# Two modulation pieces of the second block's layer 1, moved from an output projection to the feed-forward behind it

## The chip, the cores and the metric

The kernel runs on one core of one Trainium2 chip. The time of a run is the device time of one execution in microseconds, from start to end. The kernel before was timed three times: 1384.77, 1386.67 and 1389.09 us, median 1386.67 us.

## The reference, cut to what matters

Two transformer blocks in float32, batch 1, 256 tokens, width 1024. The first has causal attention and a recurrent branch, then a feed-forward. The second has two layers: layer 0 with a neighbourhood attention and a gated feed-forward, layer 1 with a latent attention and a mixture of experts. Both layers of the second block are modulated by vectors computed from a conditioning vector c:

```python
c_act = jax.nn.silu(c)
for i in range(DEPTH_2):
    mod = c_act @ w_ada[i] + b_ada[i]            # 1024 -> 6 * 1024
    sh_a, sc_a, g_a, sh_f, sc_f, g_f = jnp.split(mod, 6, axis=-1)
    h = _modulate(x, sh_a, sc_a)                 # rmsnorm(x) * (1 + sc_a) + sh_a
    m = attention of this layer (h)
    x = x + g_a * m
    h = _modulate(x, sh_f, sc_f)
    x = x + g_f * (_swiglu(h) if i == 0 else _moe(h))
```

The product `c_act @ w_ada[i]` doesn't depend on x. Its weights are 24 MB for each layer, so it may be computed at any time before the layer that uses it, as long as someone reads the weights and multiplies them.

## The kernel before, in words

**Splitting in two.** Every weight matrix comes in as float32 chunks of 1 MB (`raw`, 4 slots, loaded by SP's queue). ScalarE rounds a chunk to a high part (`whi`, line 1178) and VectorE takes the difference as a low part (`wlo`, line 1672), each in two halves. TensorE multiplies high by high, low by high and high by low (lines 681 to 683 where the weights are stationary or 694 to 698 where the activations run past them). Of `whi` and `wlo` there are two slots, so a chunk can be split only once TensorE is done with the chunk two before it.

**The modulation.** `mod` of a layer is made of 24 pieces (`ADA_CHUNKS`). Piece j is 128 rows of `w_ada` by 2048 columns (1 MB, 128 partitions by 2048), loaded by SP into one of two slots of `ada` (line 546, `load_ada`). VectorE multiplies it by a column of c and adds it to an accumulator of 128 x 2048 (`modulate_part`): the first of each eight pieces by a tensor_scalar (line 1760), the other seven by a scalar_tensor_tensor (line 1763). Pieces 0 to 7 go to `acc_first`, 8 to 15 to `acc_mid`, 16 to 23 to `acc_ends`. TensorE later sums an accumulator over partitions with one-column matmuls (line 789), and VectorE adds the bias (line 1812, `shifts`).

**What sets the order.** Nothing is planned at run time. Three tables say after which weight chunk a piece is loaded by SP and accumulated by VectorE, each entry for layer 0 and layer 1 of the second block: `ADA_MIX` for the output projection ahead of a feed-forward, `ADA_UP` for the 11 steps of the feed-forward's first product (`GU_STEPS`), and `ADA_DOWN`, the first piece that goes with the 11 chunks of its second product (`DN_CHUNKS`); all pieces from there to 23 go with one chunk each. Entry 1 is worked beside the second block's layer 0: the output projection `W_NAO` of the neighbourhood attention (4 chunks), the first product of its feed-forward `W_GU`, and the second product `W_DN2`. The result is wanted at the norm ahead of the latent attention (`norm(4, ...)`).

**SP at this place.** `load_ffn` waits for `ada_free1`, because the `ada` slots have held attention biases until the neighbourhood attention's last head is done. Then it issues the first four chunks of `W_GU` in turn, with the pieces of `ADA_MIX` among them, and goes on:

```python
if layer:
    sp.wait_ge(sem("ada_free1"), 1)
for c in range(NRAW):
    if c < len(ADA_MIX[layer]):
        load_ada(layer, ADA_MIX[layer][c])
    load(gu + c)
```

**VectorE at this place.** `down` splits a chunk and then accumulates a piece, and everything stands in one instruction stream ahead of the norm:

```python
ve.sem_inc(sem("ada_free1"), 1)
down(W_NAO, 4, 1, ADA_MIX[1], begun=1)
norm(3, halves(W_GU), halves(W_GU + 1), sc_f, sh_f, residual_gate(2, W_GU))
gate_up_silu(W_GU)
down(W_DN2, DN_CHUNKS, 1, range(ADA_DOWN[1], ADA_CHUNKS))
shifts(1, (0, 1, 3), 0, 2)
```

**The norm.** Tokens are in two tiles of 128, t = 0 and t = 1. TensorE ends an output projection with its last two chunks for t = 0 (then `tile_done`) and for t = 1. In `norm`, VectorE runs for t = 0 the gated residual (lines 1957 and 1958), splits the first half of the next stage's first chunk, waits for ScalarE's sum of squares (line 1195), and scales the rows (line 1690); ScalarE, in its own stream, splits both halves of that chunk (line 1178) ahead of the squares. TensorE turns the scaled rows by transposes (line 726). Ahead of and between the transposes of `norm(3)` and `norm(4)` stand matmuls without use (line 717, `fill`): in `norm(3)` two of them before t = 0, five between t = 0 and t = 1 and one behind; a float32 matmul shows as two rows. VectorE and ScalarE modulate the turned tiles (lines 1695 and 1207) and split them (1705 and 1213), and the first product starts.

Of the kernel before, what the change touches and what calls it, by code (L numbers as in the profile page):

```python
# [94 lines left out]
ADA_COLS = 2 * D  # L95
ADA_FIRST = KT
ADA_IN = 6
ADA_MIX = [[6, 7], [0, 1]]
ADA_UP = [{j: [7 + j] for j in range(1, 10)}, {}]
for _j in range(GU_STEPS):  # L100
    _n = 2 + _j + _j // 3
    ADA_UP[1][_j] = [_n, _n + 1] if _j % 3 == 2 else [_n]
ADA_DOWN = [ADA_UP[0][9][-1] + 1, ADA_UP[1][GU_STEPS - 1][-1] + 1]

# [147 lines left out]
def blocks(nc, a, out):  # L252

    ctx = ExitStack()
    with ctx:
# [19 lines left out]
        def sem(name):  # L275
            if name not in sems:
                sems[name] = ctx.enter_context(nc.semaphore(name))
            return sems[name]
# [240 lines left out]
        def _(sp):  # L519
            def load(c):  # L520
                ck = Chunk(c)
                if c >= NRAW:
                    sp.wait_ge(lo_done, 2 * (c - NRAW + 1))
                k, n = chunk_shape(c)
                sp.dma_start(view(raws[ck.slot], k, n), dram_chunk(c)).then_inc(raw_in[ck.slot], 16)
# [14 lines left out]
            def load_ada(layer, j):  # L540

                g = layer * ADA_CHUNKS + j
                sp.wait_ge(ada_used, g + 1)
                part, k = j // KT, j % KT
                src = a["w_ada_2"][layer][k * P:(k + 1) * P, part * ADA_COLS:(part + 1) * ADA_COLS]
                sp.dma_start(ada[:, g % NADA], src).then_inc(ada_in[g % NADA], 16)

            def load_ffn(gu, layer):
# [3 lines left out]
# [4 lines that stand above are left out]
# [1109 lines left out]
        def _(ve):  # L1665
# [47 lines left out]
            def norm(s, first, second, scale, shift=None, residual=None, between=None):  # L1713

                if s:
                    residual(0)
                    first(0)
                    normed(s, 0)
                    if s < 3:
                        first(1)  # L1720
                    residual(1)
                else:
                    normed(0, 0)
                    normed(0, 1)
                ve.wait_ge(sem("turned"), TURNED0[s] + 1)
                modulate(s, 0, 0, 4, scale, shift)
                if s:
                    normed(s, 1)
                else:
                    first(0)  # L1730
                ve.wait_ge(sem("aT_hi"), HI0[s] + 1)
                own.mark(low(0, 4, slice(0, P)))
                if between:
                    between()
                ve.wait_ge(sem("turned"), TURNED0[s] + 3)
                modulate(s, 1, 0, 2, scale, shift)
                modulate(s, 1, 2, 4, scale, shift)
                for n in range(2):
                    ve.wait_ge(sem("aT_hi"), HI0[s] + 2 + n)
                    low(2 * n, 2 * n + 2, slice(P, S)).then_inc(sem("aT_ready"), 1)  # L1740
                for n in range(2, 4):
                    ve.wait_ge(sem("aT_hi"), HI0[s] + 2 + n)
                    low(2 * n, 2 * n + 2).then_inc(sem("aT_ready"), 1)
                if not 0 < s < 3:
                    first(1)
                second(0)
                second(1)

            def halves(c):
                return lambda q: split(c, (q,))  # L1750
# [195 lines left out]
            def residual_gate(s, first):  # L1946

                gate = gate_row[(s - 2) // 2][(s - 2) % 2]

                def residual(t):  # L1950
                    if t == 0:
                        ve.wait_ge(sem("tile_done"), s + 1)
                    else:
                        ve.wait_ge(mm_done, 2 * first)
                    b = OUT_BANKS[s][t]
                    o = ps[:, b:b + 2, :].rearrange("p b n -> p (b n)")
                    own.link(ve.tensor_tensor(xn[:, t], o, gate, ALU.mult))
                    ve.tensor_tensor(x[:, t], x[:, t], xn[:, t], ALU.add).then_inc(sem("x_ready"), 1)
                return residual

            def down(first, chunks, layer=None, pieces=(), also=None, begun=0):

                for c in range(begun, chunks):
                    if also:
                        also(c)
                    if c < chunks - 2:
                        split(first + c + 2)
                    if c - begun < len(pieces):
                        modulate_part(layer, pieces[c - begun])
# [8 lines left out]

            down(W_OUT, 4, 0, ADA_MIX[0], begun=1)
            sh_a, sc_a, sh_f, sc_f = (mod[:, n * KT:(n + 1) * KT] for n in range(4))  # L1980
# [86 lines left out]
# [3 lines that stand above are left out]
# [344 lines left out]
```

## Time and profile before

| | before |
|---|---|
| median of three runs | 1386.67 us (1384.77 to 1389.09) |
| the profiled execution | 1393.49 us, of which the span is 1391.7 us |
| TensorE, matmuls | 1307.6 us busy, 94% of the span |
| VectorE | 1078.3 us busy, 77% |
| ScalarE | 834.5 us busy, 60% |
| DMA | 349.13 MB, mean 251 GB/s |
| mean granted TensorE clock | 0.967 of full speed |

The span runs from the first to the last instruction; the rest of the execution's time lies around it. Times in the rows are microseconds from the start of the span. A busy TensorE isn't TensorE at its peak, since matmuls are pipelined and overlap in the rows. The bracket behind a row tells how long the engine had been idle before it and what ended the wait.

### The profile page before, as it was taken

The numbers are of one execution on the slowest core, as the hardware profiler recorded it, in microseconds if no ns is written. First come the engines' busy times: TensorE is split into PE (matmuls) and PEld (weight loads), VectorE is DVE, ScalarE is ACT, GpSimd is POOL, SyncE is SP. The second block draws the span as 40 slices with busy tenths as digits, with TensorE's granted clock in tenths as the row PEclk, the third lists the DMA queues.
The fourth block names the chain that finished last, engine by engine and source line by source line (L and its number), as shares of the span: only waits on it lengthen the run. The fifth ranks groups of instructions, "written<-read, shape, count | busy, mean of one in ns | idle before, by whom it ended". The sixth has DMA issues, their size and how long they took to land.

```text
span 1391.7 us, 20370 instructions
## 1 busy us (share of the span) xinstructions
PE 1307.6 (94%) x7608; PEld 1141.8 (82%) x7608; DVE 1078.3 (77%) x1199; ACT 834.5 (60%) x1104; POOL 72.3 (5%) x102
## 2 busy tenths in 40 slices
PE   6989999998999799999777988999999999999996
PEld 5977999886988599998665567888888888889894
DVE  6888899878655677776635457889888888989888
ACT  5766666535655444433425655777777777777764
POOL 0010000003512000000001300000000000000000
PEclk9999999999999899999988997999999999999999
DMA  9945776699730689898232034999989998999992
GB/s 321 340 183 192 277 272 242 239 309 205 184 122 31 242 278 312 298 352 295 81 117 79 10 113 155 340 327 341 339 320 350 314 353 321 355 315 362 317 348 82
DMA packets 192890, 349.13 MB, mean 251 GB/s; under 512 B 23892, under 2 KB 161439, under 8 KB 186551
## 3 DMA queue, kind: packets, MB, share of 16 engines
q1 hardware_dynamic: 189713, 343.41, 71.9%
q10 hardware_dynamic: 2934, 4.24, 0.9%
q8 instruction: 45, 0.74, 0.2%
q0 software_dynamic: 176, 0.56, 0.1%
q14 instruction: 22, 0.18, 0.0%
HBM read 347.12 MB, written 1.06 MB: 250 GB/s over the span
## 4 chain that ended last, share of the span: by engine, by line
PE 84%; DVE 7%; ACT 5%; issue 1%; DMA 1%; POOL 0%; ACTq 0%; SPq 0%; DVEq 0%
PE ps L1143 11%; PE ps L681 8%; PE ps L682 8%; PE ps L683 8%; PE ps L1113 8%; PE ps L1115 7%; PE ps L1114 7%; PE ps L694 5%; PE ps L696 5%; PE ps L698 5%; DVE wlo L1672 1%; PE ps L1084 1%; PE ps L812 1%; PE ps L1055 1%; DVE alo L1705 1%
## 5 line engine op out<-in xcount | busy, mean ns | idle before, releaser
L1178 ACT ACTIVATE whi<-raw 128x1024 fp32r<-128x1024 f32 (+2 forms) x210 | 217.5, 1052 | 245.4 <-PE ps L683 136.3
L1672 DVE TENSOR_TENSOR wlo<-raw,whi 128x1024 fp32r<-128x1024 f32 (+2 forms) x210 | 253.0, 1229 | 117.5 <-ACT whi L1178 114.1
L681 PE MATMUL ps<-ahi,whi 128*128 128x256 f32 x960 | 276.6, 288 | 8.8 <-DVE alo L1705 8.2
L682 PE MATMUL ps<-alo,whi 128*128 128x256 f32 x960 | 273.4, 285 | 0.0
L683 PE MATMUL ps<-ahi,wlo 128*128 128x256 f32 x960 | 273.3, 285 | 0.0
L1680 DVE TENSOR_TENSOR wlo<-raw,whi 128x1792 fp32r<-128x1792 f32 (+1 forms) x96 | 199.9, 2090 | 24.6 <-ACT whi L1191 22.9
L1191 ACT ACTIVATE whi<-raw 128x1792 fp32r<-128x1792 f32 (+1 forms) x96 | 168.6, 1757 | 63.5 <-PE ps L1115 34.6
L681 PEld LDWEIGHTS ps<-ahi,whi 128*128 128x128 f32 x960 | 186.0, 194 | 14.2 <-issue 9.4
L682 PEld LDWEIGHTS ps<-alo,whi 128*128 128x128 f32 x960 | 186.0, 194 | 0.7 <-issue 0.7
L683 PEld LDWEIGHTS ps<-ahi,wlo 128*128 128x128 f32 x960 | 186.1, 194 | 0.0
L1113 PE MATMUL ps<-whi,hchi 128*128 128x448 f32 x352 | 131.4, 373 | 3.4 <-DVE hclo L2244 2.8
L1115 PE MATMUL ps<-whi,hclo 128*128 128x448 f32 x352 | 129.9, 369 | 0.0
L1114 PE MATMUL ps<-wlo,hchi 128*128 128x448 f32 x352 | 129.8, 369 | 0.0
L694 PE MATMUL ps<-whi,ahi 128*128 128x256 f32 (+3 forms) x216 | 66.2, 342 | 15.2 <-DVE wlo L1672 6.2
L1113 PEld LDWEIGHTS ps<-whi,hchi 128*128 128x128 f32 x352 | 66.7, 189 | 13.1 <-issue 4.3
L1680 DVE TENSOR_TENSOR alo<-raw,ahi 128x1792 fp32r<-128x1792 f32 (+1 forms) x32 | 66.9, 2090 | 8.3 <-ACT ahi L1191 8.3
L1115 PEld LDWEIGHTS ps<-whi,hclo 128*128 128x128 f32 x352 | 66.6, 189 | 6.0
L1680 DVE TENSOR_TENSOR wlo<-ada,whi 128x1792 fp32r<-128x1792 f32 (+2 forms) x32 | 60.5, 1891 | 14.0 <-ACT whi L1191 14.0
L1114 PEld LDWEIGHTS ps<-wlo,hchi 128*128 128x128 f32 x352 | 66.7, 189 | 5.7
L1680 DVE TENSOR_TENSOR alo<-ada,ahi 128x1792 fp32r<-128x1792 f32 (+2 forms) x32 | 60.3, 1886 | 8.6 <-ACT ahi L1191 8.6
L1191 ACT ACTIVATE ahi<-ada 128x1792 fp32r<-128x1792 f32 (+2 forms) x32 | 51.0, 1594 | 25.8 <-PE ps L1115 19.6
L696 PE MATMUL ps<-wlo,ahi 128*128 128x256 f32 (+3 forms) x216 | 64.4, 333 | 0.0
(321 smaller groups left out, 2536.7 us busy)
## 6 DMA issues: line engine op xcount, KB each, us to landing
raw<-in_moe_w_gu SPq DMA_DIRECT2D x96, 896.0 KB, 6.0
ada<-in_w_ada SPq DMA_DIRECT2D x48, 1024.0 KB, 6.9
raw<-in_moe_w_down SPq DMA_DIRECT2D x32, 1024.0 KB, 6.9
ada<-in_moe_w_gu SPq DMA_DIRECT2D x32, 896.0 KB, 6.5
raw<-in_w_up SPq DMA_DIRECT2D x22, 1024.0 KB, 5.2
raw<-in_ffn_w_gu SPq DMA_DIRECT2D x22, 1024.0 KB, 9.9
ada<-in_moe_w_down SPq DMA_DIRECT2D x16, 1024.0 KB, 7.3
raw<-in_na_w_qkv SPq DMA_DIRECT2D x12, 1024.0 KB, 7.8
```

The source lines that it names most:

```text
L681: pe.matmul(o, h[:, k, cols], bhi[:, k], start=(k == 0), stop=False)
L682: pe.matmul(o, h[:, k, cols], blo[:, k], start=False, stop=False)
L683: m = pe.matmul(o, l[:, k, cols], bhi[:, k], start=False, stop=(k == KT - 1))
L694: pe.matmul(o, bhi[at_k][:, tok], h[:, k, n0:n0 + n], start=first, stop=False)
L1113: pe.matmul(o, hchi[:, kk], h[:, k], start=(kk == 0), stop=False)
L1114: pe.matmul(o, hchi[:, kk], l[:, k], start=False, stop=False)
L1115: m = pe.matmul(o, hclo[:, kk], h[:, k], start=False, stop=(kk == KT - 1))
L1143: m = pe.matmul(ps[:, 4 + n, :], lhs[:, k0 + k], rhs[:, k, n * 512:(n + 1) * 512], start=(k0 + k == 0 and rhs is h and lhs is gchi), stop= ...
L1178: act.activation(part_of(whi[ck.half], c, q), part_of(raws[ck.slot], c, q), ACT.Copy).then_inc(hi_done, 1)
L1191: act.activation(whi[ck.half][:, 0:k * n], raws[ck.slot][:, 0:k * n], ACT.Copy).then_inc(moe_hi, 1)
L1672: ve.tensor_tensor(part_of(wlo[ck.half], c, q), part_of(raws[ck.slot], c, q), part_of(whi[ck.half], c, q).bitcast(F32), ALU.subtract).then ...
L1680: ve.tensor_tensor(wlo[ck.half][:, 0:k * n], raws[ck.slot][:, 0:k * n], whi[ck.half][:, 0:k * n].bitcast(F32), ALU.subtract).then_inc(moe_ ...
```

## The change

Pieces 0 and 1 of entry 1 leave the output projection `W_NAO`; the first product's step j now has the pieces numbered two lower, and the second product begins with piece 14 in place of 16, so it has ten pieces with its eleven chunks in place of eight.

```diff
-ADA_MIX = [[6, 7], [0, 1]]
+ADA_MIX = [[6, 7], []]
 ADA_UP = [{j: [7 + j] for j in range(1, 10)}, {}]
 for _j in range(GU_STEPS):
-    _n = 2 + _j + _j // 3
+    _n = _j + _j // 3
     ADA_UP[1][_j] = [_n, _n + 1] if _j % 3 == 2 else [_n]
 ADA_DOWN = [ADA_UP[0][9][-1] + 1, ADA_UP[1][GU_STEPS - 1][-1] + 1]
```

The instructions of TensorE, ScalarE and GpSimd stay the same and in the same order; VectorE and SP change at these places.

VectorE, between the last split of `W_NAO` and the first tile of `norm(3)` (a piece of the difference; `acc_first_66` is the accumulator of pieces 0 to 7):

```order
 L1825 TENSOR_TENSOR alo<-ps,ahi 128x256
 L1672 TENSOR_TENSOR wlo<-raw,whi 128x1024 x2
-L1760 TENSOR_SCALAR acc_first_66<-ada,vecs 128x2048
-L1763 SCALAR_TENSOR_TENSOR acc_first_66<-ada,vecs,acc_first_66 128x2048
 L1957 TENSOR_TENSOR xn<-ps,gates 128x1024
 L1958 TENSOR_TENSOR x<-x,xn 128x1024
```

The two accumulations that stood between the split and the gated residual are gone from there.

SP, from the loads of the attention's output weights on. Before:

```order
L525 DMA raw<-in_na_w_o 128x2x1024 x4
L546 DMA ada<-in_w_ada 128x2048
L525 DMA raw<-in_ffn_w_gu 128x8x256
L546 DMA ada<-in_w_ada 128x2048
L525 DMA raw<-in_ffn_w_gu 128x8x256 x3
L546 DMA ada<-in_w_ada 128x2048
```

And now:

```order
L525 DMA raw<-in_na_w_o 128x2x1024 x4
L525 DMA raw<-in_ffn_w_gu 128x8x256 x4
L546 DMA ada<-in_w_ada 128x2048
L525 DMA raw<-in_ffn_w_gu 128x8x256
L546 DMA ada<-in_w_ada 128x2048
```

The first four chunks of the feed-forward are issued one behind the other, ahead of any piece.

VectorE, the end of the second product and the start of `norm(4)`. Before:

```order
L1763 SCALAR_TENSOR_TENSOR acc_ends<-ada,vecs,acc_ends 128x2048
L1672 TENSOR_TENSOR wlo<-raw,whi 128x1024 x2
L1763 SCALAR_TENSOR_TENSOR acc_ends<-ada,vecs,acc_ends 128x2048
L1672 TENSOR_TENSOR wlo<-raw,whi 128x1024 x2
L1812 SCALAR_TENSOR_TENSOR mod<-ps,vecs 128x8 x3
L1957 TENSOR_TENSOR xn<-ps,gates 128x1024
L1958 TENSOR_TENSOR x<-x,xn 128x1024
```

And now:

```order
L1763 SCALAR_TENSOR_TENSOR acc_ends<-ada,vecs,acc_ends 128x2048
L1672 TENSOR_TENSOR wlo<-raw,whi 128x1024 x2
L1763 SCALAR_TENSOR_TENSOR acc_ends<-ada,vecs,acc_ends 128x2048 x2
L1812 SCALAR_TENSOR_TENSOR mod<-ps,vecs 128x8 x3
L1957 TENSOR_TENSOR xn<-ps,gates 128x1024
L1958 TENSOR_TENSOR x<-x,xn 128x1024
```

Two more accumulations, of pieces 22 and 23, now stand directly between the last split of the second product and the start of the next norm.

## Rows read from the trace of the kernel before

**Rows 1.** The page, part 4: the chain that ended last, by engine.
```profile
PE 84%; DVE 7%; ACT 5%; issue 1%; DMA 1%; POOL 0%; ACTq 0%; SPq 0%; DVEq 0%
```

**Rows 2.** Windows: from:to, length, busy PE, PEld, DVE, ACT, POOL, granted clock, DMA.
```profile
465.00:470.00 5.00, 0.00 (x0) 0.00 (x0) 4.56 (x5) 1.44 (x3) 0.00 (x0) 0.67 1.10 348
470.00:475.00 5.00, 4.11 (x11) 2.77 (x12) 4.43 (x8) 2.11 (x5) 0.00 (x0) 0.50 0.66 255
```

**Rows 3.** Timeline of VectorE at norm(3): start, length, instruction, idle before and releaser.
```profile
457.03 1.29 DVE L1760 TENSOR_SCALAR acc_first<-ada,vecs 128x2048 f32<-128x2048 f32 x1 [2.22 <-DMA ada<-in_w_ada]
463.59 2.35 DVE L1763 SCALAR_TENSOR_TENSOR acc_first<-ada,vecs,acc_first 128x2048 f32<-128x2048 f32 x1 [5.28 <-DMA ada<-in_w_ada]
465.86 1.22 DVE L1957 TENSOR_TENSOR xn<-ps,gates 128x1024 f32<-128x1024 f32 x1
467.11 1.22 DVE L1958 TENSOR_TENSOR x<-x,xn 128x1024 f32<-128x1024 f32 x1
```

**Rows 4.** Timeline of TensorE, end of the projection to the first product.
```profile
456.18 0.62 PE L698 MATMUL ps<-whi,alo 128*128 128x512 f32 x2
...
462.15 1.88 PE L717 MATMUL ps<-cst 128*128 128x512 f32 x4
470.89 1.97 PE L726 MATMUL ps<-cst,xn 128*128 128x128 f32 x8 [6.86 <-DVE xn L1690]
472.65 6.62 PE L717 MATMUL ps<-cst 128*128 128x512 f32 x10
479.10 1.04 PE L726 MATMUL ps<-cst,xn 128*128 128x128 f32 x8
...
481.58 0.36 PE L681 MATMUL ps<-ahi,whi 128*128 128x256 f32 x1 [0.59 <-DVE alo L1705]
```

**Rows 5.** Timeline, SP's loads at norm(3) and ScalarE, who waits for them.
```profile
452.02 0.34 SPq L546 DMA_DIRECT2D ada<-in_w_ada  x1
452.40 0.43 SPq L525 DMA_DIRECT2D raw<-in_ffn_w_gu  x1
...
461.01 2.00 ACT L1178 ACTIVATE whi<-raw 128x1024 fp32r<-128x1024 f32 x2 [6.13 <-DMA raw<-in_ffn_w_gu]
468.37 1.06 ACT L1195 ACTIVATE xn<-x 128x1024 f32<-128x1024 f32 x1 [5.36 <-DVE x L1958]
```

**Rows 6.** The page, part 6: issues, KB each, median us from issue to landing.
```profile
raw<-in_w_up SPq DMA_DIRECT2D x22, 1024.0 KB, 5.2
```

**Rows 7.** Timeline of TensorE in norm(4), and a window of the same place.
```profile
681.21 1.09 PE L726 MATMUL ps<-cst,xn 128*128 128x128 f32 x8 [0.53 <-DVE xn L1690]
687.04 1.09 PE L726 MATMUL ps<-cst,xn 128*128 128x128 f32 x8 [1.23 <-DVE xn L1690]
...
684.00:688.00 4.00, 2.77 (x12) 1.36 (x12) 2.61 (x8) 2.48 (x5) 0.00 (x0) 1.00 0.00 0
```

**Rows 8.** Windows in the first and in the second product of the feed-forward.
```profile
520.00:540.00 20.00, 20.00 (x169) 20.00 (x169) 15.88 (x15) 9.44 (x11) 0.00 (x0) 1.00 0.97 341
...
640.00:660.00 20.00, 20.00 (x88) 16.05 (x87) 17.07 (x11) 7.44 (x7) 0.00 (x0) 1.00 0.99 376
```

**Rows 9.** Timeline of VectorE at the end of the second product.
```profile
663.51 2.35 DVE L1763 SCALAR_TENSOR_TENSOR acc_ends<-ada,vecs,acc_ends 128x2048 f32<-128x2048 f32 x1
...
667.96 1.23 DVE L1672 TENSOR_TENSOR wlo<-raw,whi 128x1024 fp32r<-128x1024 f32 x1 [0.97 <-ACT whi L1178]
...
674.26 1.22 DVE L1957 TENSOR_TENSOR xn<-ps,gates 128x1024 f32<-128x1024 f32 x1 [4.85 <-PE ps L698]
675.52 1.23 DVE L1958 TENSOR_TENSOR x<-x,xn 128x1024 f32<-128x1024 f32 x1
```

**Rows 10.** Timeline of ScalarE in norm(4): the squares of tile 0.
```profile
678.71 1.04 ACT L1195 ACTIVATE xn<-x 128x1024 f32<-128x1024 f32 x1
```

**Rows 11.** Issue to landing of all pieces (first row) and of all raw chunks.
```profile
DMA to landing us min/median/max: 4.8/6.9/12.5
...
DMA to landing us min/median/max: 4.3/7.0/15.4
```

## The prediction

> **What bounds the kernel now.** I read the chain that ended last first: 84% of it is TensorE, 7% VectorE and 5% ScalarE [rows 1]. So work taken off VectorE is worth something only in the few stretches where TensorE stands still for it, and next I looked for the stretch that the change touches. The windows show it: between 465 and 470 us TensorE did nothing, and in the next window it ran at a granted clock of 0.50 [rows 2], which is 1.2 GHz, the lower of its two levels.
>
> The timelines tell who it waited for. VectorE sat idle until the first piece had landed (457.03), accumulated it, sat idle for another 5.28 us until the second had landed (463.59), and only then took up the gated residual at 465.86 [rows 3]. That residual needed nothing but TensorE's t = 0 part of the projection, whose last matmuls end at 456.18 + 0.62 = 456.8 [rows 4]. So both pieces, 3.6 us of work with the waits around them, stand on the path for about 9 us: the transposes of tile 0 begin at 470.89, and TensorE had been idle for 6.86 us [rows 4]. Then TensorE pays again: at the low clock its transposes and the five matmuls without use took until 479.10.
>
> **Part 1: the pieces leave the projection.** VectorE can begin the residual at about 456.85. The same step in norm(4) begins right behind TensorE's t = 0 part, with no piece in between [rows 9]. It ends two instructions later, 467.11 + 1.22 - 465.86 = 2.5 us [rows 3], at 459.3.
>
> Next is ScalarE, which must split both halves of the first feed-forward chunk (2.00 us) before it squares [rows 5]. That chunk landed at 461.01, 8.6 us after its issue, with one piece issued ahead of it and one behind it. Now it is issued first, at 452.02 where the piece was issued; SP's wait for the attention still stands ahead of it. When does it land? The nearest rows give: a piece at the head of the same burst, 457.03 - 452.02 = 5.0 us [rows 3, 5]; chunks of the same shape in the first feed-forward, 5.2 us median [rows 6]; and the old landing less the distance between the two old landings, 8.6 - 4.0 = 4.6 us. At the other end stands the full 8.6 to 9.0 us, if the place in the queue were worth nothing. I take 5.5 us, near the 5.2 but with some allowance for the three chunks right behind it: 457.5.
>
> Then ScalarE splits until 459.5 and squares; from its squares to the transposes took 470.89 - 468.37 = 2.5 us [rows 4, 5]. So tile 0 could be turned at 462.0. But TensorE itself is busy with t = 1 and the two fills until 462.15 + 1.88 = 464.0 [rows 4], and the next group of instructions begins 0.2 us before the last one's modelled end, as between fills and transposes at 479.10. So the transposes begin at 463.9 instead of 470.9: **7.0 us**. The cover is good for a landing until 463.9 - 2.5 - 2.0 = 459.4, 7.4 us after issue.
>
> **Part 2: the clock.** From the transposes of tile 0 to those of tile 1 it took 479.10 - 470.89 = 8.2 us, and the fills at the low clock ended that time (6.6 us for ten rows, where four rows took 1.88 at full clock, so 4.7 for ten) [rows 4]. With a TensorE that doesn't stand still for 7 us ahead of it, I take the same stretch of norm(4) as the model: 687.04 - 681.21 = 5.8 us, at clock 1.00 with gaps of 0.53 and 1.23 us [rows 7]. Its weight chunk is narrower, by about 0.2 us of ScalarE. So 6.0 us: **2.2 us** more. The bounds are 0, if the clock falls all the same, and 2.4. From tile 1 on, to the first product at 481.58, I expect the same spacing as before.
>
> A rule speaks against this part. The Trainium skill, TensorE: Matmul & The Clock Gate, section on psum-queue depth-cycling, says that short idle times between groups of matmuls can make the clock swing between its levels. By it the 2.2 us would not come and the sum would be 7.0. The row of norm(4) speaks against the rule here, so it is a rival and no more.
>
> **Part 3: the feed-forward's first product.** It has the same number of pieces in each step, numbered two lower. Step 0 gets a first piece of eight (1.29 us) where it had a 2.35 us one. TensorE is busy 20.00 of 20.00 us in this stage and VectorE 15.9 [rows 8], so this is worth 0. The loads keep their places in SP's queue, except that chunks 0 to 3 come one or two transfers earlier and the first piece lands behind them; it is wanted only some 9 us after the first product has begun. If this cover were gone, the price would be the 2.35 us of one piece.
>
> **Part 4: the second product.** Ten chunks carry a piece instead of eight. Per chunk TensorE needs 5.6 us and VectorE 2.4 + 2.35 = 4.8, so VectorE keeps up; in the window with a piece for every chunk TensorE is busy all the time, at 376 GB/s [rows 8]. Two chunks more at that rate cost 0. The first chunk carries a 2.35 us piece instead of a 1.28 us one, with two chunks of lead: 0.
>
> The end is the delicate place. Piece 22 follows the last split at 667.96 + 1.23 = 669.2 and ends at 671.5. Piece 23 is loaded when piece 21 has freed its slot, which is at 663.51 + 2.35 = 665.9 [rows 9]. With the fastest landing of a piece, 4.8 us, it is there at 670.7, ahead of its turn; with the median of 6.9 us at 672.8 [rows 11]. So it is accumulated by 673.8 or by 675.1. Behind it stand the small shift sums, some 0.5 us, and the residual, which began at 674.26 [rows 9]. That residual has room: ScalarE takes up the squares only at 678.71, when it has split the next chunk [rows 10], and the residual ended at 675.52 + 1.23 = 676.75, so there are 2.0 us of slack. The cost is 0 for both landings. At the longest landing, 12.5 us [rows 11], it is 678.4 + 2.35 + 0.5 = 681.2 against the 676.2 allowed: 5.0 us. I take 0: only one chunk stands ahead of this piece in the queue, issued when the chunk two before it was split, one 5.6 us step earlier.
>
> **The sum.** 7.0 + 2.2 + 0 + 0 = 9.2 us. No other stage starts by the clock on the wall, so what is won is carried to the end. The profiled execution took 1393.49 us around a span of 1391.7; I expect 1384.3 of it. The three timed runs have their median at 1386.67, 6.8 us below the profiled one, and reach over 4.3 us. I take the same 9.2 us off that median: **1377.5 us**. A measurement can tell about 0.3%, 4.2 us, from no change.
>
> **The rivals.**
>
> A. **The chunk is what keeps the norm, not the piece.** If the order in the queue is worth nothing, it still lands at 461.0, and the transposes begin at 461.0 + 2.0 + 2.5 = 465.5: 5.4 us, with the clock 7.6 us. For it: ScalarE did wait 6.13 us for it, and three 1 MB chunks follow it at once. Against it: 4.0 us lay between the landings of the piece and of the chunk, so the queue does work mostly in order. Result 1379 to 1381 us. One page bears on the size: the Trainium skill, DMA: Bandwidth & Descriptors, table of specifications, gives line rate from 512 bytes on, so by it the chunk with its 1 KB rows should land as fast as the piece, at 457.0; the 4.0 us between the two landings are rather more than one megabyte at the measured 348 GB/s (3.0 us).
>
> B. **The clock doesn't stay up.** The transposes begin at 463.9 but tile 1 follows 8.2 us later: 7.0 us, 1379.7 us. For it: the norm remains a place with short gaps, and the rule above. Against it: norm(4).
>
> C. **The time is won at norm(3) and mostly given back in front of norm(4)**, by a late piece 23 of 5.0 us as worked out above: net 4.2 us or less, 1382.5 us or more. For it: in the second product the DMA share is 0.99 [rows 8], and pieces have taken up to 12.5 us. Against it: those long landings came in bursts like the one at 452.
>
> D. **Slower.** The same mechanism with a heavier price: VectorE runs in order, so the shift sums, both residuals and the splits for the latent attention are queued behind its wait for piece 23, and TensorE waits for them. With a landing of 15.4 us, the longest of any weight chunk [rows 11], the residual begins at 684.1, 7.9 us late. TensorE then stands still long enough to fall to the low clock as it did at 465, which cost 0.9 us on the transposes and 1.9 on the fills: 10.7 us against 9.2, so 1388 us. It decides from a landing of about 14 us on. Nothing in rows of this stage is near that.
>
> **How the numbers follow.** The forecast (8 to 10.5 us won) has a chance of 0.62. A has 0.12 and B 0.12; both are still faster by more than 0.3%. C and the case that no gain shows at the end at all have 0.10, D has 0.04. So: faster 0.86, within 0.3% 0.10, slower 0.04. The range goes from 1374.0, which is a gain of 10.5 us and the 2 us by which the lowest timed run lies under the median, to 1382.5, where C begins; it takes in A and B.
>
> **What would show it.** In the changed profile the residual at line 1957 begins near 456.9 and line 1763 no longer stands ahead of it; ScalarE's wait for the chunk ends near 457.5; the transposes (726) follow at 463.9 and 469.9 with a clock of 1.00 between them; the first product begins at 472.3. At the end of the second product two accumulations follow the last split, and the squares of norm(4) begin as far behind TensorE's t = 1 part as before. I am wrong if ScalarE's wait ends past 459.4 (A), if tile 1 follows tile 0 by 8 us (B), or if the residual of norm(4) begins more than 2 us behind tile_done (C, D).

## The result, and the profile after

The changed kernel takes 1380.94 us (median), the kernel before 1388.17 us in the same series: a ratio of 0.9939, 95% interval 0.9923 to 0.9955. The ratio leaves out one slow run of the changed kernel (1622.28 us at a granted clock of 0.741). By the ratio that is 8.5 us less, by the two medians 7.2; forecast were 9.2 us and a time of 1377.5. A second series gave 0.9938 (0.9915 to 0.9961). The profiled execution of the changed kernel took 1380.68 us around a span of 1378.9.

Two profiled executions also differ where nothing was changed: in this one the projection ahead of norm(3) ends 2.8 us sooner than in the one shown before (the first fill at 459.37 instead of 462.15), since the clock was a little higher between 300 and 400 us. The two spans lie 12.8 us apart, which is more than the times show: 2.8 us of it lie ahead of norm(3), 8.9 between its first fill and tile 1 of norm(4), and 1.1 behind that. So I read everything from the first fill of norm(3) on, the first row of line 717. The timeline of TensorE in the changed kernel (start, length, instruction, idle before and releaser) answers to [rows 4]:

```profile
459.37 1.88 PE L717 MATMUL ps<-cst 128*128 128x512 f32 x4
461.32 1.09 PE L726 MATMUL ps<-cst,xn 128*128 128x128 f32 x8
462.25 4.46 PE L717 MATMUL ps<-cst 128*128 128x512 f32 x10
467.31 1.09 PE L726 MATMUL ps<-cst,xn 128*128 128x128 f32 x8 [0.60 <-DVE xn L1690]
...
469.85 0.36 PE L681 MATMUL ps<-ahi,whi 128*128 128x256 f32 x1 [0.59 <-DVE alo L1705]
```

From the first fill to the transposes of tile 0 it is now 1.95 us, where it was 8.74; from those to the transposes of tile 1 it is 5.99 us, where it was 8.21; and on to the first product 2.54, where it was 2.48. Together 10.48 us instead of 19.43, so 8.95 us less. The ten rows of five fills take 4.46 us instead of 6.62: the clock.

What VectorE, ScalarE and SP do there, three timelines of the changed kernel and the landing of the first chunk (last row: KB, us from issue to landing), answers to [rows 3, 5]:

```profile
454.06 1.23 DVE L1957 TENSOR_TENSOR xn<-ps,gates 128x1024 f32<-128x1024 f32 x1 [1.99 <-PE ps L698]
455.32 1.23 DVE L1958 TENSOR_TENSOR x<-x,xn 128x1024 f32<-128x1024 f32 x1
...
456.91 2.01 ACT L1178 ACTIVATE whi<-raw 128x1024 fp32r<-128x1024 f32 x2 [4.78 <-PE ps L698]
458.82 1.04 ACT L1195 ACTIVATE xn<-x 128x1024 f32<-128x1024 f32 x1
...
449.27 5.22 SPq L525 DMA_DIRECT2D raw<-in_ffn_w_gu  x4
...
raw<-in_ffn_w_gu SPq DMA_DIRECT2D x1, 1024.0 KB, 5.2
```

The residual no longer waits for a landing but for TensorE's t = 0 part. The thing to see is the second bracket: ScalarE's split, which used to wait 6.13 us for the chunk's landing, now waits for TensorE (4.78 <-PE). The chunk has landed at 449.27 + 5.2 = 454.5, 2.4 us before the split, but the slot of `whi` that ScalarE writes is still being read. And the residual is over at 456.55, 2.3 us before ScalarE takes its squares at 458.82.

The window from 465 to 470 us, in which TensorE had done nothing before, answers to [rows 2]; its columns are the same (the clock is the third number from the end):

```profile
465.00:470.00 5.00, 3.81 (x15) 1.71 (x15) 3.21 (x8) 2.99 (x8) 0.00 (x0) 1.00 0.02 10
```

The end of the second product, timelines of VectorE, ScalarE and TensorE, answers to [rows 7, 9, 10]:

```profile
656.25 1.23 DVE L1672 TENSOR_TENSOR wlo<-raw,whi 128x1024 fp32r<-128x1024 f32 x1 [0.97 <-ACT whi L1178]
657.40 4.80 DVE L1763 SCALAR_TENSOR_TENSOR acc_ends<-ada,vecs,acc_ends 128x2048 f32<-128x2048 f32 x2
662.12 0.30 DVE L1812 SCALAR_TENSOR_TENSOR mod<-ps,vecs 128x8 f32<-128x8 f32 x3
662.57 1.23 DVE L1957 TENSOR_TENSOR xn<-ps,gates 128x1024 f32<-128x1024 f32 x1
...
667.00 1.04 ACT L1195 ACTIVATE xn<-x 128x1024 f32<-128x1024 f32 x1
...
669.50 1.09 PE L726 MATMUL ps<-cst,xn 128*128 128x128 f32 x8 [0.53 <-DVE xn L1690]
675.33 1.09 PE L726 MATMUL ps<-cst,xn 128*128 128x128 f32 x8 [1.23 <-DVE xn L1690]
```

Pieces 22 and 23 run back to back in 4.80 us, so piece 23 had landed: it was issued at 654.17 and took 4.9 us, so it was there at 659.1, some 0.7 us before its turn. The residual has lost its wait for TensorE (4.85 us before), but begins as far ahead of the first fill of norm(4) as before, 5.38 us against 5.40. The transposes of tile 1 follow those of tile 0 after 5.83 us, as before. From the first product of the feed-forward to the transposes of norm(4) it is 199.65 us (469.85 to 669.50), before it was 199.63. From the first fill in norm(3) to tile 1 in norm(4) the kernel has gained 8.9 us (215.96 instead of 224.89). The second pair of traces has 10.65 us there (214.38 instead of 225.03); the 1.7 us more are scatter of the clock in the second product, of which the last section tells.

### The profile page after: what moved, and what is told of

It reads as the page before. It is cut to its first block, busy times and chain, and to the rows that moved or that the text cites. A ratio compares the mean times of both kernels' runs of the same rounds, so it can differ in the third digit from the quotient of the medians.

```text
span 1378.9 us, 20370 instructions
## 1 busy us (share of the span) xinstructions
PE 1301.3 (94%) x7608; PEld 1138.0 (83%) x7608; DVE 1078.2 (78%) x1199; ACT 834.8 (61%) x1104; POOL 73.7 (5%) x102
## 4 chain that ended last, share of the span: by engine, by line
PE 86%; DVE 6%; ACT 5%; issue 1%; POOL 0%; DMA 0%; ACTq 0%; DVEq 0%
PE ps L1143 11%; PE ps L681 8%; PE ps L682 8%; PE ps L683 8%; PE ps L1113 8%; PE ps L1115 8%; PE ps L1114 8%; PE ps L694 6%; PE ps L696 5%; PE ps L698 5%; PE ps L1084 1%; DVE wlo L1672 1%; PE ps L812 1%; PE ps L1055 1%; PE ps L1091 1%
## 5 line engine op out<-in xcount | busy, mean ns | idle before, releaser
L1191 ACT ACTIVATE ahi<-raw 128x1792 fp32r<-128x1792 f32 (+1 forms) x32 | 56.1, 1752 | 12.8 <-PE ps L1143 6.7
```

What stands on the lines that cost most here:

```text
L1191: act.activation(whi[ck.half][:, 0:k * n], raws[ck.slot][:, 0:k * n], ACT.Copy).then_inc(moe_hi, 1)
```

## The experiments

**One piece at a time, and loads apart from work.** The first four kernels change one thing each. Pieces 0 and 1 loaded as before, but accumulated in the feed-forward (changed kernel, SP's part of the code):

```diff
                 for c in range(NRAW):
-                    if c < len(ADA_MIX[layer]):
+                    if layer and c < 2:
+                        load_ada(layer, c)
+                    elif c < len(ADA_MIX[layer]):
                         load_ada(layer, ADA_MIX[layer][c])
                     load(gu + c)
...
+                        if layer == 0 or n > 1:
                             load_ada(layer, n)
```

> Changed kernel, but pieces 0 and 1 are still LOADED among the first four chunks, as before; VectorE accumulates them in the feed-forward. I read the distance from the first use-less matmul (line 717) of norm(3) to the first product (line 681): 19.4 us before, 10.5 us in the changed kernel. Theory 1, the gain came from VectorE's order, and the place in the queue costs only what the chunk lands later: ScalarE gets its first chunk about 1.3 us later than TensorE's slot allows (1.1 us ahead of the first fill instead of 2.5), so 11.8 us, total gain against before 7.6 us. Rival, the queue place was what mattered: the loads are as before, so the distance stays above 16 us and the gain under 4 us.

Measured: ratio 0.9957 (0.9939 to 0.9975). In its trace (lines are numbered 3 higher) ScalarE and TensorE show:

```profile
459.53 2.00 ACT L1181 ACTIVATE whi<-raw 128x1024 fp32r<-128x1024 f32 x2 [6.38 <-DMA raw<-in_ffn_w_gu]
...
460.39 1.88 PE L720 MATMUL ps<-cst 128*128 128x512 f32 x4
463.94 1.09 PE L729 MATMUL ps<-cst,xn 128*128 128x128 f32 x8 [1.67 <-DVE xn L1693]
```

The first product follows the first fill after 12.08 us (472.47), near the 11.8 of theory 1. So in the changed kernel the old place of the loads costs 1.6 us of the 8.95, through the chunk that then lands 8.8 us after its issue; the order on VectorE is the other 7.3. The clock stays up behind an idle time of 1.67 us. All this is read from the trace: the interval of the time overlaps that of the changed kernel, here and in the next two experiments.

The work without the loads (changed kernel, VectorE):

```diff
             down(W_NAO, 4, 1, ADA_MIX[1], begun=1)
+            xf, c0 = x.rearrange("p t n -> p (t n)"), vec("c")[:, 0:1]
+            own.link(ve.tensor_scalar(acc_first1, xf, c0, None, ALU.mult))
+            own.link(ve.scalar_tensor_tensor(acc_first1, xf, c0, acc_first1, ALU.mult, ALU.add))
```

> Changed kernel plus two operations on VectorE at the old place of the pieces, of the same size and kind (tensor_scalar and scalar_tensor_tensor, 128 x 2048, 3.6 us together), which read x and need no load; their result is overwritten later and used by nothing, so this kernel does 3.6 us more work than needed. Theory 1, it was the wait for the landing that cost and not the work: VectorE had been idle 2.0 us ahead of the residual, and the residual ended 2.3 us before ScalarE took it, so the work fits: distance from the first fill to the first product 10.5 to 10.8 us, time as the changed kernel (ratio 0.994). Rival, the work itself stands on the path: 3.6 less 2.0 us of idle time and more, so 12.1 to 14.1 us and a ratio of 0.995 to 0.997.

Measured: ratio 0.9949 (0.9926 to 0.9972), and 10.48 us from the first fill (462.30) to the first product (472.78), to the hundredth what the changed kernel has. Here the residual begins 1.6 us later against TensorE (3.68 us ahead of the first fill instead of 5.31), ScalarE splits and squares where it did:

```profile
458.62 1.22 DVE L1957 TENSOR_TENSOR xn<-ps,gates 128x1024 f32<-128x1024 f32 x1
...
459.84 2.01 ACT L1178 ACTIVATE whi<-raw 128x1024 fp32r<-128x1024 f32 x2 [4.78 <-PE ps L698]
461.76 1.04 ACT L1195 ACTIVATE xn<-x 128x1024 f32<-128x1024 f32 x1
```

So 3.6 us of work at that place cost nothing when it waits for no load. What the change took away was the wait for the landings.

Half of the change, piece 0 left in the projection:

```diff
-ADA_MIX = [[6, 7], [0, 1]]
+ADA_MIX = [[6, 7], [0]]
...
-    _n = 2 + _j + _j // 3
+    _n = 1 + _j + _j // 3
```

> Half of the change: piece 0 stays in the output projection, piece 1 and all behind it are one place on instead of two. Theory 1: piece 0 lands 5.0 us after its issue, about 5.1 us ahead of the first fill, and its 1.3 us are over long before ScalarE is ready; what is left is the first chunk behind one transfer, 1.1 us ahead of the fill: distance first fill to first product 11.8 us against 10.5 and 19.4, gain 7.6 us of the 8.9. Rival, each piece bears half of the cost: 15 us, gain 4.5 us.

Measured: ratio 0.9959 (0.994 to 0.9977); first fill 461.22, first product 473.23, so 12.01 us. Piece 0 is accumulated at 456.14 and the residual follows at 457.34; ScalarE waits for its chunk until 460.30. The first piece costs only the transfer ahead of the chunk. The second one costs 7.4 us of the 8.95. It stands in the queue behind a piece and a chunk; how much of its cost comes from that place, a kernel further down shows.

**The clock by itself.** Kernel before, with fills over the wait:

```diff
-FILL = {1: (1, 3, 1), 2: (2, 7), 3: (2, 5, 1), 4: (1, 2), 5: (1, 4)}
+FILL = {1: (1, 3, 1), 2: (2, 7), 3: (9, 5, 1), 4: (1, 2), 5: (1, 4)}
```

> Kernel before, with nine use-less matmuls instead of two while TensorE waits for the pieces in norm(3): the wait stays, but TensorE isn't idle in it. Theory 1, 2.2 us of the 8.9 were the clock: the distance from the first fill to the transposes of tile 0 stays 8.7 us, from those to tile 1 it falls from 8.2 to 6.0 us, at a granted clock of 1.00; total distance 17.2 us instead of 19.4. Rival, the stretch is long for another reason (VectorE's late residual of tile 1): it stays at 8.2 us and nothing is won.

Measured: in the trace 17.31 us from the first fill (460.71) to the first product (478.02), with 5.99 us from tile 0 to tile 1; but the time showed no gain, 1.0008 (0.9989 to 1.0027). The same kernel was measured once more:

> The same kernel as e4_fills_bridge (kernel before, the wait in norm(3) filled with use-less matmuls), whose trace had 2.1 us less in norm(3) and whose time showed no gain. Theory 1, scatter hid it: ratio 0.9985. Rival, the clock part of the gain isn't there in timed runs: 1.000 or more.

This time 0.9988 (0.997 to 1.0005), and 17.64 us in the trace (462.48 to 480.12). Its windows show the low clock gone though VectorE waits as before:

```profile
465.00:470.00 5.00, 5.00 (x13) 2.09 (x11) 4.97 (x4) 0.92 (x1) 0.00 (x0) 1.00 1.10 348
470.00:475.00 5.00, 3.77 (x15) 2.08 (x15) 4.53 (x9) 2.80 (x8) 0.00 (x0) 1.00 0.75 283
```

Both traces show the 1.8 to 2.1 us. The two timed ratios lie on either side of no change, and 2.1 us is 0.0015, about as much as their intervals reach to either side; the times don't show this part of the gain.

**Was the landing or the slot the bound?** The first three chunks ahead of SP's wait, in the changed kernel and, with pieces 0 and 1 directly behind that wait, in the kernel before:

```diff
-                if layer:
-                    sp.wait_ge(sem("ada_free1"), 1)
-                for c in range(NRAW):
-                    if c < len(ADA_MIX[layer]):
+                ahead = NRAW - 1 if layer else 0
+                for c in range(ahead):
+                    load(gu + c)
+                if layer:
+                    sp.wait_ge(sem("ada_free1"), 1)
+                    for n in ADA_MIX[layer]:
+                        load_ada(layer, n)
+                for c in range(ahead, NRAW):
+                    if layer == 0 and c < len(ADA_MIX[layer]):
                         load_ada(layer, ADA_MIX[layer][c])
                     load(gu + c)
```

> Changed kernel, but SP issues the first three chunks of the feed-forward ahead of its wait for the attention (they need only free raw slots), not behind it. Theory 1, ScalarE's first split waits for TensorE to free the slot of whi and not for the landing: ScalarE still begins 2.5 us ahead of the first fill, first fill to first product stays 10.5 us, nothing is won. Rival, the landing is the bound (as I predicted it): ScalarE begins up to 4 us sooner, the transposes follow the fills at once, distance 10.2 us.

Measured: ratio 0.9931 (0.9905 to 0.9957), within its interval the same as the changed kernel. The trace decides: SP issues the first chunk at 443.26, which is 21.05 us ahead of the first fill instead of 10.10, and it lands 5.2 us later. Still ScalarE's split begins only at 461.85, as before 2.46 us ahead of the first fill (464.31), with the same bracket, 4.78 <-PE. Fill to product is 10.47 us. The landing isn't the bound.

> Kernel BEFORE with its pieces in the old place on VectorE, but the first three chunks issued ahead of SP's wait, then pieces 0 and 1 directly one behind the other. Theory 1, the 7 us were the wait for piece 1, which stood behind piece 0 and a chunk in one queue: now it lands one transfer earlier, about 2.8 us behind piece 0, so 2.4 us ahead of the first fill instead of 1.4 us behind it. The residual begins at the fill, ends 2.5 us later, and the transposes follow 2.5 us after that: 5.0 us behind the first fill instead of 8.7; then 6.0 us if the clock holds: distance first fill to first product 13.5 to 15.7 us, against 19.4 before and 10.5 changed, ratio 0.996 to 0.9975. Rival, VectorE's order is all that counts and the place in the queue nothing: 18 us or more.

Measured: ratio 0.9996 (0.9978 to 1.0014). VectorE and TensorE in this kernel (lines 5 higher):

```profile
457.37 1.29 DVE L1765 TENSOR_SCALAR acc_first<-ada,vecs 128x2048 f32<-128x2048 f32 x1 [2.19 <-DMA ada<-in_w_ada]
461.08 2.35 DVE L1768 SCALAR_TENSOR_TENSOR acc_first<-ada,vecs,acc_first 128x2048 f32<-128x2048 f32 x1 [2.42 <-DMA ada<-in_w_ada]
...
462.50 1.88 PE L722 MATMUL ps<-cst 128*128 128x512 f32 x4
468.37 1.97 PE L731 MATMUL ps<-cst,xn 128*128 128x128 f32 x8 [3.99 <-DVE xn L1695]
470.13 6.40 PE L722 MATMUL ps<-cst 128*128 128x512 f32 x10
```

Piece 1 lands 3.7 us behind piece 0, not 2.8 as I had said, so 1.4 us ahead of the fill; the transposes come 5.87 us behind it, and TensorE's idle time of 3.99 us is enough for the low clock. The distance is 16.36 us, 3.1 us less than before but outside the 13.5 to 15.7 of theory 1; the rival's 18 us didn't come either. The time shows no gain: its interval ends at 3.1 us. So by the trace 3.1 of the 7.4 us of piece 1 came from its place in the queue, and 4.3 stay even directly behind piece 0 (16.36 against the 12.01 with piece 0 alone). Better order in the queue helps, but can't replace taking the pieces off the path.

**How much more the second product can carry.** One more piece moved there (changed kernel):

```diff
-    _n = _j + _j // 3
-    ADA_UP[1][_j] = [_n, _n + 1] if _j % 3 == 2 else [_n]
+    _n = _j + _j // 3 - 1
+    ADA_UP[1][_j] = [_n, _n + 1] if _j % 3 == 2 else [_n] if _j else []
```

> Changed kernel, with one more piece moved on: the feed-forward's first step has none, and the second product has 11 pieces with its 11 chunks, so that three accumulations follow the last split ahead of norm(4). This tests the cover that the prediction claimed there: the residual has 2.0 us of slack. Piece 23 is now loaded when piece 21 is done, which is 2.35 us behind the last split; with a landing of 4.8 to 6.9 us it lands about 7.2 to 9.3 us behind that split, against the 5.0 us or so at which TensorE ends t = 0. Theory 1: the residual begins 10 to 12 us behind the last split instead of 5.1, and after taking off 2.0 us of slack tile 0's transposes are 3 to 5 us late: ratio 0.9965 to 0.998. Rival, loads land fast enough in a queue that is empty there (4.8 us or less, nothing ahead), and only the 2.35 us of work count: 0 to 0.5 us late, ratio as the changed kernel.

Measured: ratio 0.9979 (0.996 to 0.9998), so by the two ratios 5.6 us of the gain are lost again; their intervals reach 2.2 and 2.6 us to either side. VectorE, then TensorE, then windows of norm(4):

```profile
657.55 4.81 DVE L1763 SCALAR_TENSOR_TENSOR acc_ends<-ada,vecs,acc_ends 128x2048 f32<-128x2048 f32 x2
665.16 2.35 DVE L1763 SCALAR_TENSOR_TENSOR acc_ends<-ada,vecs,acc_ends 128x2048 f32<-128x2048 f32 x1 [2.81 <-DMA ada<-in_w_ada]
...
667.88 1.23 DVE L1957 TENSOR_TENSOR xn<-ps,gates 128x1024 f32<-128x1024 f32 x1
...
668.11 1.02 PE L717 MATMUL ps<-cst 128*128 128x512 f32 x2
672.92 1.97 PE L726 MATMUL ps<-cst,xn 128*128 128x128 f32 x8 [3.79 <-DVE xn L1690]
...
681.51 1.44 PE L726 MATMUL ps<-cst,xn 128*128 128x128 f32 x8
...
672.00:676.00 4.00, 3.08 (x15) 3.08 (x16) 3.93 (x7) 1.07 (x4) 0.00 (x0) 0.51 0.00 0
676.00:680.00 4.00, 4.00 (x13) 2.97 (x14) 1.89 (x5) 3.06 (x7) 0.00 (x0) 0.50 0.00 0
```

Piece 23 is issued at 659.93 and lands at 665.16, 5.2 us later. Tile 0's transposes begin 4.81 us behind the end of the projection instead of 1.55, so 3.3 us late, inside the 3 to 5 us that I had expected. But tile 1 follows after 8.59 us instead of 5.83: the idle time of 3.79 us brought the low clock, and another 2.8 us. Together 6.0 us, and the time agrees (5.6). In this one trace 3.1 us of them come back elsewhere: from the first product to the first fill of norm(4) it takes 194.96 us, in the changed kernel 198.10, since the clock never falls in the second product here. I had left the clock out of this expectation, though my rival D had it in.

**Beyond the change.** Squares of tile 0 ahead of the split of the chunk, on ScalarE and likewise on VectorE, and no fills ahead of tile 0 in norm(3) and norm(4). The core of the edit:

```diff
+                if s in (3, 4):
+                    act.wait_ge(sem("x_ready"), NT * (s - 1) + 1)
+                    square(s, 0, x[:, 0])
+                    first(0)
+                    first(1)
...
                     residual(0)
-                    first(0)
+                    if s not in (3, 4):
+                        first(0)
                     normed(s, 0)
+                    if s in (3, 4):
+                        first(0)
...
-FILL = {1: (1, 3, 1), 2: (2, 7), 3: (2, 5, 1), 4: (1, 2), 5: (1, 4)}
+FILL = {1: (1, 3, 1), 2: (2, 7), 3: (0, 5, 1), 4: (0, 2), 5: (1, 4)}
```

> Changed kernel; in norm(3) and norm(4) ScalarE takes the squares of tile 0 ahead of the split of the next chunk, VectorE scales the rows of tile 0 ahead of its part of that split, and the use-less matmuls ahead of the transposes of tile 0 go (2 in norm(3), 1 in norm(4)). Theory 1, in the changed kernel the transposes of tile 0 are kept by two things that end together: TensorE's own fills (0.2 us before them) and ScalarE's split, which waits for TensorE's slot and not for the landing. With both gone they can begin right behind tile 1's part of the projection: in norm(3) 1.9 us earlier, in norm(4) 1.5 us (1.55 us between the projection's end and the transposes before), tile 1 follows 6.0 and 5.8 us later; sum 3.4 us against the changed kernel, ratio to before 0.991 to 0.992. Rival, the chain behind tile 0 takes it back, since both tiles need the same ScalarE work in all and the split is only moved behind: tile 1 follows 7 to 8 us later, gain 0 to 1 us. Second rival, without the fills the clock falls: slower than the changed kernel by 1 us or more.

> The same kernel as e5_squares_first, beside the changed kernel on one chip. Its trace had 8.5 us from the end of the projection to the first product in norm(3) (10.5 in the changed kernel) and 5.8 us from the end of the projection to tile 1 in norm(4) (7.4), so 3.6 us less. Theory 1: the time follows, ratio 0.0025 below that of the changed kernel in the same series, 0.991. Rival, the low clock behind norm(4) takes it back: ratio within 0.001 of the changed kernel's.

Measured: 0.9932 (0.9909 to 0.9955) the first time, 0.9905 (0.9884 to 0.9926) the second, median 1377.27 us, where the changed kernel had 0.9938 and 1381.46 us in that second series. The second trace:

```profile
462.28 1.03 PE L726 MATMUL ps<-cst,xn 128*128 128x128 f32 x8
463.15 4.46 PE L717 MATMUL ps<-cst 128*128 128x512 f32 x10
468.20 1.09 PE L726 MATMUL ps<-cst,xn 128*128 128x128 f32 x8 [0.59 <-DVE xn L1696]
...
470.74 0.36 PE L681 MATMUL ps<-ahi,whi 128*128 128x256 f32 x1 [0.58 <-DVE alo L1711]
...
667.24 1.04 PE L726 MATMUL ps<-cst,xn 128*128 128x128 f32 x8
673.01 1.09 PE L726 MATMUL ps<-cst,xn 128*128 128x128 f32 x8 [1.23 <-DVE xn L1696]
```

The transposes of tile 0 follow the projection without a gap in both norms, and tile 1 follows 5.92 and 5.77 us later, at full clock: neither rival of the first expectation came. From the end of the projection to the first product it is 8.46 us in norm(3) instead of 10.48, and in norm(4) 5.77 us to tile 1 instead of 7.38 (667.95 to 675.33): 3.6 us. The second series has both kernels side by side and shows a difference of 0.0033, or 4.6 us (by the medians 4.2): six runs of this kernel between 1375.22 and 1378.82 us, six of the changed one between 1378.19 and 1384.22. The first time it was only 0.0007, against a measurement of the changed kernel in another series. The intervals of the ratios overlap narrowly, so the traces show the size of this gain more surely than the times do.

**Controls.** The kernel before and the changed kernel again:

> The kernel before, unchanged, as a control. So far the timed gains lie some 20% under those read in the traces between the first fill of norm(3) and the tile 1 transposes of norm(4) (changed kernel 8.5 of 8.95 us, one piece 5.7 of 7.4, bridged wait -1.1 of 2.1). Theory 1, that is scatter: ratio 1.000 with an interval that holds 1, and the second trace has the same 19.4 us from first fill to first product. Rival, the first trace of the kernel before was an unlucky one: 17 us here.

> The changed kernel, unchanged, for a second and closer measurement. Theory 1, the 8.95 us of the trace are what the time gains: ratio 0.9925 to 0.995. Rival, part of it is given back outside the stretch: ratio above 0.995.

Measured: 0.9999 (0.9982 to 1.0015) and 0.9938 (0.9915 to 0.9961). The traces repeat to 0.15 us: 19.56 us from first fill to first product before (461.89 to 481.45), 10.47 us changed (462.38 to 472.85). The control's rival, a first trace that happened to be long, is out. By the ratio the changed kernel gains 8.6 us here, so its time doesn't lag behind the 8.95 of the trace by more than the interval allows (5.4 to 11.8 us).

## Why the prediction was right, and where it wasn't

**Part 1**, tile 0's transposes 7.0 us sooner: measured 6.8 (8.74 less 1.95). The landing was right too: 5.2 us after issue, forecast were 5.5. The step that failed comes behind it: "Then ScalarE splits until 459.5 and squares". It lets the split begin as soon as the chunk is there, and it doesn't. ScalarE waits for TensorE to finish the t = 1 pass over the chunk that holds the slot of `whi`, and begins 2.46 us ahead of the first fill, where I had said 4.65. In the time of the kernel before that is 459.7, against 459.4, the last moment that I had said TensorE's own work would cover. So my sign for rival A, a wait that ends past 459.4, did come, for another reason than A gives. The cover was missed by 0.3 us, and the transposes begin 1.95 us behind the first fill instead of 1.75. That the 7.0 came out so well is luck in part: nothing in my working kept the slot from coming free later. The kernel with the loads among the chunks shows the price, since there ScalarE begins 1.6 us later against the first fill and the first product comes 1.6 us later too. The condition on the slot stands in the description of the kernel, and norm(4) shows ScalarE squaring only after the next chunk's split. I used that for the slack in Part 4 but didn't ask in Part 1 what the split itself waits for once its data is there.

**Part 2**, tile 1 after 6.0 us instead of 8.2: measured 5.99. The stretch of norm(4) was the right model. The kernel that only bridges the wait has the same 5.99 us with the pieces still in place, so these 2.2 us are the clock and nothing else in the traces. The times of that kernel don't show them. The Trainium skill, TensorE: Matmul & The Clock Gate, section on psum-queue depth-cycling, tells of a kernel whose clock swings because TensorE often stands still for a short time between groups of matmuls. In norm(3) that wasn't borne out: gaps of 0.6, 1.2 and 1.67 us left the clock at 1.00. In norm(4) it isn't ruled out, since in one trace the clock fell there with no longer gap than 0.53 us, as the last section shows.

**Part 3**, nothing in the first product: 199.65 us to norm(4) against 199.63. The second trace of the changed kernel has 198.09, that of the kernel before 199.65; the last section shows this 1.6 us as scatter of the clock.

**Part 4**, nothing at the end of the second product: piece 23 was there 0.7 us before its turn, and the residual began as far ahead of norm(4)'s first fill as before (5.38 us, was 5.40), though now directly behind VectorE's own work. The 2.0 us of slack are real; the kernel with one more piece went past them and paid 3.3 us for being late and 2.8 us for the clock. So rivals C and D named the right place, and the change stops one piece short of it.

**The sum**: 9.2 us forecast, 8.9 in the traces, 8.5 by the ratio of the times and 7.2 by their medians. The first series can't tell these apart: its interval is 6.2 to 10.7 us. The predicted 1377.5 us was taken off a median of 1386.67; the longer series puts the kernel before at 1388.17, and 9.2 us off that is 1379.0 against 1380.94.

**Rival A** had its premise wrong: the place in the queue is worth 3.4 us, since the chunk lands 5.2 us after its issue at the head and landed 8.6 us after it before. It was right that the chunk can become the bound, and it does when its load stands behind the pieces (12.08 us instead of 10.48); this was taken away along with the pieces. **Rival B** didn't come.

## What to carry to other kernels

Before work that isn't urgent stands in front of urgent work on an engine, ask whether its data will be there: here 3.6 us of extra work in that place cost nothing, and a piece that had to be waited for cost 7.4 us, the clock included. When such a wait is removed, ask of every instruction behind it what it will wait for next; a busy buffer slot looks like nothing in the old trace. And price a stall of TensorE with the low clock behind it: of 8.95 us here 2.2 were clock, and of the 6.0 that one piece too many cost, 2.8.

## What the runs showed of the hardware that I had not expected

An idle time of 1.67 us before the transposes left TensorE at full clock; with 3.79 and 3.99 us it fell to half, and stayed there through the transposes and most or all of the fills behind them.

A short idle time doesn't make sure of the full clock. In the norm(4) of the kernel with the loads among the chunks the last gap was 0.53 us, 16 one-column matmuls of the modulation sums followed, and then the fills took 3.63 us instead of 1.96; tile 1 came 0.3 us later for it (6.13 us behind tile 0 instead of 5.83):

```profile
670.52 1.09 PE L729 MATMUL ps<-cst,xn 128*128 128x128 f32 x8 [0.53 <-DVE xn L1693]
671.45 1.87 PE L792 MATMUL ps<-cst,acc_ends 128*128 128x1 f32 x16
673.19 3.63 PE L720 MATMUL ps<-cst 128*128 128x512 f32 x4
```

The clock also falls without any idle time. At the 32 one-column matmuls of the modulation sums in the second product (line 789) TensorE is busy all the time, and during them or shortly behind them it falls to 0.50. For how long differs from run to run: some 7 us in the first changed trace and in both of the kernel before, some 3 us in the second changed trace, not at all in that of the kernel with one more piece. Whether these matmuls are the cause wasn't tried. Windows of this stretch in the changed kernel and in the kernel with the loads among the chunks:

```profile
600.00:650.00 50.00, 50.00 (x219) 40.97 (x218) 35.47 (x26) 16.88 (x18) 0.00 (x0) 0.93 0.81 294
```

```profile
600.00:650.00 50.00, 50.00 (x229) 40.94 (x228) 36.85 (x27) 18.33 (x18) 0.00 (x0) 0.97 0.82 305
```

From the first product to norm(4) the one needs 199.65 us and the other 198.05. The two changed-kernel traces differ by the same amount (199.65 and 198.09), so 1.6 us of the scatter of single executions come from this one place.

At the head of the queue a piece (rows of 8 KB) landed after 5.0 us and a chunk (rows of 1 KB) after 5.2. Two pieces issued directly one behind the other landed 3.7 us apart, where I had reckoned with 2.8, while a piece behind a chunk landed 2.6 us after it, and a chunk behind a piece 4.0 to 4.2 us. What makes the difference wasn't tried.
